# Output projection's weights issued ahead of the residual, key copies moved from VectorE to ScalarE, and the last half finished by token tiles, in a two-layer hybrid decoder

## The reference

```python
def layer(x, l, ...):
    h = rms_norm(x, g_ffn1_pre[l])
    x = x + 0.5 * rms_norm(swiglu(h, w_ffn1_in[l], w_ffn1_out[l]), g_ffn1_post[l])
    mix, ... = mix_layer(rms_norm(x, g_mix_pre[l]), ...)
    x = x + rms_norm(mix, g_mix_post[l])
    h = rms_norm(x, g_ffn2_pre[l])
    return x + 0.5 * rms_norm(swiglu(h, w_ffn2_in[l], w_ffn2_out[l]), g_ffn2_post[l])
```

## Time and profile before

| | |
|---|---|
| median of 3 runs | 2396.93 us (2396.19 to 2397.25) |
| the profiled execution's own time | 2383.74 us |
| its span in the trace | 2382.1 us |
| mean granted clock of TensorE | 0.978 of full |
| TensorE (PE) busy | 2262.2 us (95%) |
| VectorE (DVE) busy | 1198.0 us (50%) |
| ScalarE (ACT) busy | 925.7 us (39%) |
| GpSimd (POOL) busy | 146.3 us (6%) |
| DMA | 290.97 MB, mean 122 GB/s |

### The profile page before, as it was taken

How to read it: one execution, slowest core, us unless ns; L and a number is a source line. 1 busy time by engine, 2 the same in 40 slices (tenths; PEclk the granted TensorE clock), 3 DMA queues, 4 the chain that set the end, 5 groups by cost and what they waited for, 6 DMA issues and landing times. The chain is left out here.

```text
span 2382.1 us, 44896 instructions
## 1 busy us (share of the span) xinstructions
PE 2262.2 (95%) x17646; PEld 2056.9 (86%) x17646; DVE 1198.0 (50%) x2114; ACT 925.7 (39%) x1637; POOL 146.3 (6%) x197
## 2 busy tenths in 40 slices
PE   7999999999898899999999999999998898999997
PEld 7999999777656699999999999987775667999997
DVE  6434265426666565432454333762467664743425
ACT  6223342324426654323352233432244474622333
POOL 0000010002222000000000000100113300000000
PEclk8999999999989999999999999999999998999999
DMA  5223334216867632232323333441468755422333
GB/s 141 78 70 88 103 104 136 87 64 188 265 184 212 208 107 72 80 96 77 102 73 95 82 88 89 123 131 53 125 197 255 243 150 184 104 74 70 91 104 93
DMA packets 384958, 290.97 MB, mean 122 GB/s; under 512 B 51808, under 2 KB 368393, under 8 KB 384273
## 3 DMA queue, kind: packets, MB, share of 16 engines
q1 hardware_dynamic: 368128, 234.08, 34.7%
q0 software_dynamic: 16128, 54.54, 7.3%
q10 hardware_dynamic: 528, 0.02, 0.0%
HBM read 274.99 MB, written 13.58 MB: 121 GB/s over the span
## 5 line engine op out<-in xcount | busy, mean ns | idle before, releaser
L222 PE MATMUL ps<-h_hi,w_hi 128*128 128x288 f32 x2400 | 716.8, 299 | 16.0 <-PEq L177 10.3
L223 PE MATMUL ps<-h_lo,w_hi 128*128 128x288 f32 x2400 | 708.5, 295 | 0.0
L224 PE MATMUL ps<-h_hi,w_lo 128*128 128x288 f32 x2400 | 708.2, 295 | 0.0
L222 PEld LDWEIGHTS ps<-h_hi,w_hi 128*128 128x128 f32 x2400 | 450.5, 188 | 23.3 <-issue 16.6
L246 DVE TENSOR_TENSOR w_lo<-w_raw,w_hi 128x2048 fp32r<-128x2048 f32 x143 | 327.7, 2292 | 260.9 <-ACT w_hi L240 260.5
L223 PEld LDWEIGHTS ps<-h_lo,w_hi 128*128 128x128 f32 x2400 | 450.7, 188 | 1.0
L224 PEld LDWEIGHTS ps<-h_hi,w_lo 128*128 128x128 f32 x2400 | 450.6, 188 | 0.0
L240 ACT ACTIVATE w_hi<-w_raw 128x2048 fp32r<-128x2048 f32 x143 | 272.9, 1908 | 129.0 <-PE ps L224 77.5
L222 PE MATMUL ps<-f_a_hi,w_hi 128*128 128x288 f32 x1024 | 302.7, 296 | 0.0
L224 PE MATMUL ps<-f_a_hi,w_lo 128*128 128x288 f32 x1024 | 301.6, 295 | 0.0
L223 PE MATMUL ps<-f_a_lo,w_hi 128*128 128x288 f32 x1024 | 301.5, 294 | 0.0
(11 more groups left out here) (365 smaller groups left out, 3203.4 us busy)
## 6 DMA issues: line engine op xcount, KB each, us to landing
w_raw<-in_w_ffn_in SPq DMA_DIRECT2D x132, 512.0 KB, 5.2
w_raw<-in_w_ffn_out SPq DMA_DIRECT2D x80, 512.0 KB, 4.5
sa_vn<-in_cache_sb_v SPq DMA_DIRECT2D x256, 128.0 KB
w_raw<-in_w_in SPq DMA_DIRECT2D x52, 512.0 KB, 4.4
sa_vn<-in_cache_win_v SPq DMA_DIRECT2D x96, 128.0 KB
w_raw<-in_w_out SPq DMA_DIRECT2D x24, 512.0 KB, 8.1
sa_kn_early<-in_cache_win_k POOLq DMA_DIRECT2D x72, 128.0 KB
sa_vn<-in_cache_win_v SPq DMA_DIRECT2D x16, 512.0 KB
```

Of the source, the lines that this page charges most:

```text
L222: pe.matmul(out, stat_hi, mov_hi, start=start, stop=False, skip_group_check=True)
L223: pe.matmul(out, stat_hi, mov_lo, start=False, stop=False, skip_group_check=True)
L224: return pe.matmul(out, stat_lo, mov_hi, start=False, stop=stop, skip_group_check=True)
```

## The change

1. `output`: the transfer of `x` is issued inside `post_sync`, behind the loads of visit 3, and VectorE's wait for it moves from ahead of `post_vector` to its second half, ahead of the first operation that touches `x`.
2. Mixing: `copy_keys_b` is gone from VectorE; ScalarE copies the second bank right behind the first, in every tick.
3. Ending stage: the second half is finished by token tiles (96, 128 and 64 tokens, all eight chunks in one operation), with `inv` broadcast over the chunks and the product written over `Y`; TensorE may turn a tile as soon as it is whole (`x_whole`). ScalarE copies all turned banks but the second of tile 0 and of tile 4, which VectorE copies.
4. Beginning stage: ScalarE takes both halves of tile 3 and the first of tile 4, VectorE the second of tile 4; the `page_rows` operations go ahead of the first `split_lo`.

```diff
@@ def post_sync(...)
+        if behind and v == 3:
+            behind()
@@ def post_vector(...)
     dve.wait_ge(S["pre_gain_loaded"], 16)
+    if x_loaded is not None:
+        dve.wait_ge(x_loaded, 16)
     for q in range(first + 1, len(units)):
@@ def output(...)
-            sp.dma_start(E["X"].rearrange("p c n -> p (c n)"), E["spill"]).then_inc(S["x_loaded"], 16)
             sp.wait_ge(S["part_lo"], 1)
-            post_sync(sp, S, E, I["w_out"], l, KC, 0, 2, 1, load_next)
+
+            def load_x():
+                sp.dma_start(E["X"].rearrange("p c n -> p (c n)"), E["spill"]).then_inc(S["x_loaded"], 16)
+
+            post_sync(sp, S, E, I["w_out"], l, KC, 0, 2, 1, load_next, load_x)
...
-            dve.wait_ge(S["x_loaded"], 16)
-            post_vector(dve, E, S, St, F, KC, 0, 1, "mix", Jt)
+            post_vector(dve, E, S, St, F, KC, 0, 1, "mix", Jt, S["x_loaded"])
@@ copy_keys_a(act, n)
         act.activation(kt[:, n % 2, 0], ps[:, TURN_A[e % len(TURN_A)], :], ACT.Copy).then_inc(S["free_a"], 1)
+        act.wait_ge(S["turned_b"], ev_b["k", n] + 1)
+        act.activation(kt[:, n % 2, 1], ps[:, TURN_B[ev_b["k", n] % len(TURN_B)], :], ACT.Copy).then_inc(S["free_b"], 1)
@@ vector_tick(dve, t)
-        if t < U:
-            copy_keys_b(dve, t)
@@ beginning: scalar
-            turned(range(HALF_TILES, TILES))
+            for t in range(HALF_TILES, TILES):
+                for half in range(2 if t < PT_TILES else 1):
+                    act.wait_ge(S["turned"], 2 * t + half + 1)
+                    out, src = turned_view(t, half)
+                    act.activation(out, src, ACT.Copy).then_inc(S["act_out"], 1)
@@ beginning: vector
+            dve.wait_ge(S["rows_loaded"], 16 * DEC_BATCH + 16)
+            dve.tensor_copy(wide[:], E["page_rows"][:]).then_inc(S["widened"], 1)
+            dve.wait_ge(S["widened"], 1)
+            dve.tensor_scalar(E["page_rows"][:], wide[:], PAGE // SG, lane[:, 0:1], ALU.mult, ALU.add)
             split_lo(dve, S, E, 0, 1)
...
-            turned(range(HALF_TILES, TILES))
...
+            turned(range(PT_TILES, TILES))
@@ ending_stage: tensor
-                pe.wait_ge(So["x_new"], len(J.late) if t < ready else len(J.open.tiles))
+                if t < ready:
+                    pe.wait_ge(So["x_new"], len(J.late))
+                else:
+                    pe.wait_ge(S["x_whole"], t - ready + 1)
@@ ending_stage: scalar
-            turned(range(TILES))
+            for t, half in order:
+                if (t, half) not in by_vector:
+                    act.wait_ge(S["turned"], 2 * t + half + 1)
+                    dst, src = turned_view(t, half)
+                    act.activation(dst, src, ACT.Copy).then_inc(S["act_out"], 1)
@@ ending_stage: vector
-            turned(range(ready))
+            turned(0, 1)
             y_inverse(dve, So, 1)
-            fin_vector(dve, E, So, F, J.open, J.second, False)
-            turned(range(ready, TILES))
+            for n, t in enumerate(range(ready, TILES)):
+                at = slice(max(HALF, t * P), t * P + ROWS[t])
+                yv, xv = E["Y"][:, :, at], E["X"][:, :, at]
+                dve.tensor_tensor(yv, yv, E["inv"][:, at].unsqueeze(1).to_broadcast([P, KC, at.stop - at.start]),
+                                  ALU.mult).then_inc(S["y_scaled"], 1)
+                dve.wait_ge(S["y_scaled"], n + 1)
+                dve.tensor_tensor(xv, xv, yv, ALU.add).then_inc(S["x_whole"], 1)
+            turned(TILES - 1, 1)
```

## The result

The changed kernel takes 2372.31 us in the median of 4 runs (2366.88 to 2374.73), the kernel before, beside it, 2396.56 us (2395.98 to 2397.25). The ratio is 0.9905, with a 95% interval of 0.9881 to 0.9929: 22.8 us faster (between 17 and 29). The forecast was 2374.3 us.

The account below looks back on a forecast made before the run. PE at 95% busy was taken to bound the kernel, so time lay in its idle stretches and low clock. Terms -11.2 - 6.0 - 4.5 - 0.9 = -22.6 us gave 2374.3 us for the median, range 2363 to 2386.

Parts of the forecast that it names:

- Weights ahead: Output projection: third weight block loaded without the residual ahead of it removes PE's `w_lo` wait and half clock; -11.2 us.
- The cover: Output projection: the residual, issued behind the fourth block, lands before 838, ahead of its reader at 853.22 or 848.8.
- Rival (C): Output projection gains nothing because the third block lands late for another reason; 2385.5 us, chance 0.10.
- Key copies: Mixing: moving 104 copies from VectorE to ScalarE shortens PE's waits, net 3.0 us per layer, -6.0 us.
- the 0.5 per layer: Mixing: one mLSTM product waiting for ScalarE just behind a copy grows by 0.5 us, against 3.6 gained per layer.
- rival (E): Mixing: fewer idle stretches leave PE at full clock more often, four waits losing a tail; 2367.5 us, chance 0.07.
- Because ScalarE idles more than half of this stretch: Mixing: reason given for taking -6.0 us, near the lower end between -13.8 and +61 us.
- Ending: Ending stage: six wide VectorE operations instead of 16, with PE turning each tile once whole; -4.5 us.
- the cut by tokens: Ending stage: finishing by token tiles lets PE start after two of six operations; expected to be worth 3.0 us.
- Beginning: Beginning stage: one more copy on ScalarE and page rows ahead of the split end it earlier; -0.9 us.
- I find no part of the program that explains this: Whole kernel: median 2396.93 us is 13.2 above the profiled execution's 2383.74; differences were taken over to the median unchanged.
- the low end: Whole kernel: mixing at -13.8 us and 1.1 for the ending stage give 2365.4, with half a clock tail 2363 us.

## Why the prediction was right, and where not

The total is nearer than the terms. -22.6 was forecast, and -22.8 by the ratio and -23.0 by the stages were measured, but term by term the stages give -9.4, -9.2, -4.2 and -0.2 for -11.2, -6.0, -4.5 and -0.9: one term too small by 3.2 covers three that were too large by 2.8 in sum. That they cancel to 0.4 is luck, and a second measurement of the same kernel gave 0.9891, 26 us.

- **Weights ahead**: the mechanism and its two halves hold (no wait for `w_lo`, full clock behind). The size, 9.4 us by the stages, is 1.8 less than forecast: layer 0 gives 4.2 for 4.40, layer 1 5.2 for 6.76. The step at fault took layer 1's price from the one profile in which that stretch was longest of six (71.4 us, mean 70.4): there and in one other the clock stood at 0.50 for 6.8 us behind the wait, in the other four for 3.4. The cover held: the residual, issued at 825.62, took 11 us and landed near 837 (838 at the latest was forecast), and its reader stood at 850.87. Rival (C), a block that lands late for another reason, is out.
- **Key copies**: mis-sized, 8 to 13 us for 6.0. The waits removed were those named, and their price was right, 3.6 and 3.4 us for 3.6 per layer. Over all profiles, what PE leaves unfilled fell by only 4.0 us in sum, below the 6.0: the 0.5 per layer that I allowed for what comes back was the step that failed. ScalarE's key copies alone took back 0.9 per layer, which I had put at next to nothing, and the mLSTM's decays 0.4. A mean of 5.2 us of clock came on top, which the sum had left out and rival (E) has.
- **"Because ScalarE idles more than half of this stretch"**: this reason for taking the low price was weak. Another set of copies costs 30% of its time, so busy share does not say how much an engine is felt.
- **Ending**: right in size (4.2 for 4.5) and in each duration; the cut by tokens was worth 1.9 for the 3.0 that I had expected of it, and the 1.1 between them is the clock.
- **Beginning**: 0.2 us for 0.9. VectorE's list does end earlier, at 21.41 instead of 22.05, and PE's first product of the FFN comes 0.63 sooner in these two profiles and 0.7 sooner in the means of 5 and 8 (22.6 for 23.3). What I had left out is the clock there. The FFN begins at half clock either way, and the clock rises where it does, not with the first product:

```profile
23.06 0.58 PE L222 MATMUL ps<-h_hi,w_hi 128*128 128x288 f32 x1 [5.04 <-PEq L177]
...
26.05 0.29 PE L222 MATMUL ps<-h_hi,w_hi 128*128 128x288 f32 x1
```

and with the change:

```profile
22.43 0.58 PE L222 MATMUL ps<-h_hi,w_hi 128*128 128x288 f32 x1 [3.78 <-PEq L177]
...
26.14 0.29 PE L222 MATMUL ps<-h_hi,w_hi 128*128 128x288 f32 x1
```

  Time won ahead of the rise is spent at half clock and worth half. Since the rise also came 0.4 us later in the mean of the profiles with the change, 0.2 is left.
- **Profile and median**: "I find no part of the program that explains this" was the weakest sentence. Between the two profiles the part is the mixing of layer 1. That the total did not suffer from it is again luck in part: the gains were taken over as differences, but layer 1's output projection was priced from that one execution, and the mixing's clock stood in no term of the sum.
- **Two readings**: PE does stand idle above 0.1 us inside some products of the FFNs and projections (0.2 to 0.4 us, at four places such as 898.7), which changes nothing in the sum. And by its own terms the low end would be 2362, not 2363 (2365.4 less half of 6.8).

## What to carry to other kernels

Price a change in a stage that comes out alike in every execution from one profile, but look at a second profile of the unchanged kernel before pricing one in a stage whose length depends on the granted clock. When a transfer is put back in a queue, its waiting reader must be put back as well: half of that edit cost 0.4% here, both halves won 0.3%. To learn what an engine's work in a tight weave is worth, double it: this showed that PE feels VectorE's copies about twice as much as ScalarE's (68% and 30%), though the doubled price is no measure of what removal gives.

## What the runs showed of the hardware that was not expected

- Executions of one kernel differ by up to 23 us (2384.44 to 2407.17 in 35 runs), and the slower ones have the lower mean clock. Between the two that were profiled, nearly all of the difference is time at half clock in one stage (18.7 and 42.5 us), with waits that are equal in sum (35.6 and 34.9 us).
- Time won ahead of a rise of the clock is worth half: at the head of the first FFN PE began 0.63 us sooner, at half clock, and once the clock had risen it was 0.30 sooner (its product at L359 at 27.33 for 27.63).
- At the head of the output projection identity products from 817.27 on, behind 1.87 us without work, did not keep the clock up: it was at 0.50 from 817 to 820. It was back at full sooner (0.95 over 820 to 823, where the changed kernel has 0.50), but by then the products had cost as much.
